# Rounded single-pass masks and gate sums, and the logits of two attention maps issued together, in a four-layer fp32 kernel

## The reference

```
logit[i, j] = q_i . k_j + c_i - c_j   for j <= i, masked above;  c = cumsum(log sigmoid(x w_f + b_f))
out = softmax(logit) v * silu(gate)
```

```
s[c] = scale * q[c] k[c]^T, masked above;  p[c] = softmax(s[c])
out = rmsnorm((p[0] - lam * p[1]) v) * (1 - lam0) * silu(z)
```

## Time and profile before

| | |
|---|---|
| median of 3 runs | 3882.92 us |
| the 3 runs | 3876.78, 3882.92, 3889.24 us |
| profiled execution, its time | 3884.34 us |
| profiled execution, its span | 3882.5 us |
| mean granted clock of TensorE | 0.961 |
| TensorE busy (matmul) | 3566.0 us, 92% |
| VectorE busy | 2130.9 us, 55% |
| ScalarE busy | 1293.7 us, 33% |
| instructions | 43173 |

### The profile page before, as it was taken

How to read it: one execution, slowest core, us unless ns; L and a number is a source line. 1 busy time by engine, 2 the same in 40 slices (tenths; PEclk the granted TensorE clock), 3 DMA queues, 4 the chain that set the end, 5 groups by cost and what they waited for, 6 DMA issues and landing times.

```text
span 3882.5 us, 43173 instructions
## 1 busy us (share of the span) xinstructions
PE 3566.0 (92%) x16018; PEld 2837.7 (73%) x16018; DVE 2130.9 (55%) x3127; ACT 1293.7 (33%) x2014; POOL 150.5 (4%) x100
## 2 busy tenths in 40 slices
PE   7899999978889999999989999998899999999899
PEld 6677777757667888878877777686677877677667
DVE  6655545555555555534343665476655466566664
ACT  4233323334323223333232224424333223432432
POOL 2000000000002000000031000000002000000000
PEclk9899999989989999999999999999999999999899
DMA  4233334445555555655543443334346343334345
GB/s 151 94 115 115 104 118 140 152 149 180 177 200 198 181 167 184 202 173 195 171 149 104 139 141 121 108 125 149 127 138 232 116 154 130 103 120 148 127 133 190
DMA packets 286129, 574.59 MB, mean 148 GB/s; under 512 B 61392, under 2 KB 101088, under 8 KB 285408
## 3 DMA queue, kind: packets, MB, share of 16 engines
q1 hardware_dynamic: 285920, 571.83, 44.2%
HBM read 440.65 MB, written 131.07 MB: 147 GB/s over the span
## 4 chain that ended last, share of the span: by engine, by line
PE 45%; issue 22%; DVE 16%; ACT 7%; DMA 6%; DVEq 2%; POOLq 1%; SPq 1%; ACTq 0%
PE bank L541 29%; PE bank L540 9%; DVE weights_low L466 4%; ACT weights_high L393 3%; DMA arena<-in_s_bc 2%; DVE arena L1947 1%; POOLq L452 1%; ACT arena L1889 1%; PE bank L2224 1%; PE bank L1064 1%; DVE arena L1811 1%; DMA arena<-fm_b 1%; DMA residual_in<-x_part 1%; DVE act_low L524 1%; PE bank L972 1%
## 5 line engine op out<-in xcount | busy, mean ns | idle before, releaser
L541 PE MATMUL bank<-act_high,weights_high 128*128 128x512 f32 x3584 | 1464.9, 409 | 62.4 <-DVE stream_out L513 27.5
L541 PE MATMUL bank<-act_low,weights_high 128*128 128x512 f32 x3584 | 1428.2, 398 | 0.0
L466 DVE TENSOR_TENSOR weights_low<-weights_raw,weights_high 128x1024 fp32r<-128x1024 f32 x528 | 656.7, 1244 | 1282.2 <-ACT weights_high L393 1279.9
L393 ACT ACTIVATE weights_high<-weights_raw 128x1024 fp32r<-128x1024 f32 x528 | 557.8, 1057 | 1608.2 <-PE bank L541 1336.5
L541 PE MATMUL bank<-act_high,weights_low 128*128 128x512 f32 x3584 | 964.6, 390 | 0.0
L541 PEld LDWEIGHTS bank<-act_high,weights_high 128*128 128x128 f32 x3584 | 696.7, 194 | 232.3 <-issue 38.6
L541 PEld LDWEIGHTS bank<-act_low,weights_high 128*128 128x128 f32 x3584 | 694.6, 194 | 142.4 <-issue 3.6
L541 PEld LDWEIGHTS bank<-act_high,weights_low 128*128 128x128 f32 x3584 | 673.9, 188 | 140.9
L540 PE MATMUL bank<-weights_high,act_high 128*128 128x512 f32 x640 | 257.7, 403 | 23.1 <-DVE stream_out L479 18.0
L540 PE MATMUL bank<-weights_high,act_low 128*128 128x512 f32 x640 | 252.5, 395 | 0.0
L2021 DVE SCALAR_TENSOR_TENSOR residual_in<-residual_in,arena 128x512 f32<-128x512 f32 x240 | 180.3, 751 | 20.2 <-issue 1.2
(11 more groups left out here) (314 smaller groups left out, 3043.7 us busy)
## 6 DMA issues: line engine op xcount, KB each, us to landing
weights_raw<-in_w_all SPq DMA_DIRECT2D x528, 512.0 KB, 3.4
convert_in<-mix SPq DMA_DIRECT2D x80, 256.0 KB, 4.0
fm_b<-stream_out SPq DMA_DIRECT2D x72, 256.0 KB, 2.3
mix<-arena SPq DMA_DIRECT2D x64, 256.0 KB, 4.2
x_part<-stream_out SPq DMA_DIRECT2D x48, 256.0 KB, 2.2
residual_in<-x_part SPq DMA_DIRECT2D x12, 1024.0 KB, 6.4
x<-stream_out SPq DMA_DIRECT2D x48, 256.0 KB, 2.6
convert_in<-x SPq DMA_DIRECT2D x48, 256.0 KB, 3.9
```

The lines of the kernel that those rows point to most:

```text
L393: e.activation(WH[:, t % 3, :], RAW[:, t % 3, :], ACT.Copy).then_inc(wh_ready, 1)
L466: e.tensor_tensor(WL[:, t % 3, :], RAW[:, t % 3, :], WH[:, t % 3, :].bitcast(F32), ALU.subtract).then_inc(wl_ready, 1)
L541: return e.matmul(bank[s][:, :], a[:, s * P:(s + 1) * P], h, start=start, stop=stop)
```

## The change

- The mask and the identity that carries it get rounded copies (`CAUSAL_R`, `IDENT_R`, type fp32r), made once by two ScalarE copies in the third unit; TensorE waits for them there. The mask's fill value becomes -2^100, which rounding keeps. All mask matmuls use the copies.
- The gate sums are kept on partitions 64 to 71 and 96 to 103 instead of 32 to 39, and stage `forget` splits them: rounded sums on the first group of partitions, the remainder on the second (`fx_cr`). A rounded selector for each head (`fx_head`) takes the place of the matrix of ones, so the product picks the head's row and adds both parts in one fp32r matmul. The multiplication L1441 and the semaphore step "row" go, and one of two memsets.
- In the differential attention both maps' q by k of a block are issued one behind the other, then both masks.
- Storage: `fx_cr` and `fx_head` lie in the buffer of the small weights, whose next filling waits for the last `fox` logits; the rotary tables are loaded into the start of `at_w`.

The diff:

```diff
@@ constants
-NEG = -1e30
+NEG = -2.0 ** 100
-        CAUSAL = sb("causal", [P, P])
+        IDENT_R = sb("ident_rounded", [P, P], F32R)
+        CAUSAL_R = sb("causal_rounded", [P, P], F32R)
...
@@ small_act
+            if i == 1:
+                e.wait_ge(*fx_p.at("lc", 7))
             e.activation(SMW[:, :, 0:64], small_raw, ACT.Copy).then_inc(*sm_a.mark("high"))
@@ fox: steps and buffers
-        fx_d = steps("fx_dve", "row m3 m2 m0 p3 p2 p0 m1 p1 mix")
+        fx_d = steps("fx_dve", "m3 m2 m0 p3 p2 p0 m1 p1 mix")
-        fx_row, fx_cum = A(L), A(L)
+        fx_cum = A(L)
-        FR = slice(32, 40)
+
+        FR, LOW = slice(64, 104), slice(96, 104)
+
+        fx_head, fx_cr = SMW[:, 0:8, :], two_d(SMW[:, 8:12, :])
@@ forget_dve
-            e.memset(fx_row, 0.0)
             e.memset(fx_one, 1.0)
...
             e.tensor_tensor_scan(fx_cum[FR, :], fx_one[FR, :], fx_t1[FR, :], 0.0, ALU.mult, ALU.add)
+            e.drain()
+            e.tensor_scalar(fx_cr, SMO[:, :], 0.0, None, ALU.mult)
+            e.drain()
+            e.tensor_copy(fx_cr[FR, :], fx_cum[FR, :])
+            e.tensor_copy(fx_head, fx_pick.rearrange("p (h o) -> p h o", o=1).broadcast_to([P, 8, P]))
+            e.drain()
+            e.tensor_tensor(fx_cr[LOW, :], fx_cum[LOW, :], fx_cr[LOW, :].bitcast(F32), ALU.subtract)
             e.drain().then_inc(*fc_d.mark("done"))
@@ fox_pe
                 e.matmul(out[:, :n], fx_q[:, b * P:n], fx_k[:, :n], start=True, stop=False)
-                e.matmul(out[:, :n], ONES[:, :], fx_row[:, :n], start=False, stop=False)
-                return e.matmul(out[:, b * P:n], IDENT[:, :], CAUSAL[:, :], start=False, stop=True)
+                e.matmul(out[:, :n], fx_head[:, h, :], fx_cr[:, :n], start=False, stop=False)
+                return e.matmul(out[:, b * P:n], IDENT_R[:, :], CAUSAL_R[:, :], start=False, stop=True)
...
-            e.wait_ge(*fx_d.at("row", h))
+            if h == 0:
+                e.wait_ge(*fc_d.at("done"))
@@ fox_dve
-            if h:
-                e.wait_ge(*fx_p.at("lc", h - 1))
-            else:
-                e.wait_ge(*fc_d.at("done"))
-            e.tensor_scalar(fx_row[FR, :], fx_cum[FR, :], fx_pick[FR, h:h + 1], None, ALU.mult).then_inc(*fx_d.mark("row"))
@@ attention
-        at_cos, at_sin = A(TB, 32), A(TB, 32)
+
+        at_cos, at_sin = (at_w[:, 0, 128 * n:128 * n + 128].rearrange("p (b d) -> p b d", b=TB) for n in range(2))
@@ att_pe
-            def logits(b, c, out):
-                w, r = (b + 1) * P, slice(64 * c, 64 * c + 64)
-                e.matmul(out[:, :w], at_q[r, b * P:w], at_k[r, :w], start=True, stop=False)
-                return e.matmul(out[:, b * P:w], IDENT[:, :], CAUSAL[:, :], start=False, stop=True)
+
+            def logits(b, outs):
+                w = (b + 1) * P
+                for c, out in enumerate(outs):
+                    r = slice(64 * c, 64 * c + 64)
+                    e.matmul(out[:, :w], at_q[r, b * P:w], at_k[r, :w], start=True, stop=False)
+                return [e.matmul(out[:, b * P:w], IDENT_R[:, :], CAUSAL_R[:, :], start=False, stop=True) for out in outs]
...
-            for c in range(2):
-                logits(3, c, mid[c]).then_inc(*p.mark(f"l3{c}"))
-            for c in range(2):
-                logits(2, c, mid[2 + c])
-                logits(0, c, mid[2 + c][:, 3 * P:]).then_inc(*p.mark(f"l2{c}"))
+            for c, mm in enumerate(logits(3, mid[0:2])):
+                mm.then_inc(*p.mark(f"l3{c}"))
+            logits(2, mid[2:4])
+            for c, mm in enumerate(logits(0, [x[:, 3 * P:] for x in mid[2:4]])):
+                mm.then_inc(*p.mark(f"l2{c}"))
...
-            for c in range(2):
-                mm = logits(1, c, mid[c])
-            mm.then_inc(*p.mark("l1"))
+            logits(1, mid[0:2])[1].then_inc(*p.mark("l1"))
@@ constants, ScalarE and TensorE at the third unit
                 if t == 2:
                     e.wait_ge(const_in, 80)
+                    e.activation(IDENT_R[:, :], IDENT[:, :], ACT.Copy)
+                    e.activation(CAUSAL_R[:, :], OUTB[:, 3, 0:P], ACT.Copy).then_inc(mask_ready, 1)
...
                 if t == 2:
                     e.wait_ge(const_in, 80)
+                    e.wait_ge(mask_ready, 1)
                 unit_pe(e, t)
```

More of the change, by code:

```diff
@@ L222, in build @@
         TRI = sb("tri", [P, P])
-        CAUSAL = sb("causal", [P, P])
+        IDENT_R = sb("ident_rounded", [P, P], F32R)
+        CAUSAL_R = sb("causal_rounded", [P, P], F32R)
         GAIN = sb("norm_gains", [P, 6, KT])
         GLUB = sb("glu_bias", [P, KT])
-        ARENA_N = 20040
+        ARENA_N = 19920
         ARENA = sb("arena", [P, ARENA_N])
@@ L256, in build @@
         out_stored, xr_in, zr_in = sem("out_stored"), sem("xr_in"), sem("zr_in")
-        const_in, gain_in = sem("const_in"), sem("gain_in")
+        const_in, gain_in, mask_ready = sem("const_in"), sem("gain_in"), sem("mask_ready")
         cv_in = [sem(f"cv_in{c}") for c in range(4)]
@@ L2543, in _ @@
             weights_sp(e, 2)
-            for dst, src in ((IDENT, "ident"), (TRI, "tri"), (CAUSAL, "causal"), (ONES, "ones"), (GLUB, "glu_b")):
-                e.dma_start(dst[:, :], I[src]).then_inc(const_in, 16)
+            for dst, src in ((IDENT[:, :], "ident"), (TRI[:, :], "tri"), (OUTB[:, 3, 0:P], "causal"), (ONES[:, :], "ones"), (GLUB[:, :], "glu_b")):
+                e.dma_start(dst, I[src]).then_inc(const_in, 16)
             for n in BY_SLOT[0]:
@@ L2676, in layout @@
     fb = np.zeros((P, 8), np.float32)
-    fb[32:40, 0] = v["fox_f_b"][0]
+    fb[64:72, 0] = fb[96:104, 0] = v["fox_f_b"][0]
     out["fox_b"] = fb
     pick = np.zeros((P, 8), np.float32)
-    pick[32:40] = np.eye(8)
+    pick[64:72] = pick[96:104] = np.eye(8)
     out["fox_pick"] = pick
     fold = np.zeros((P, P), np.float32)
-    fold[32:40, 32:40] = fold[96:104, 32:40] = np.eye(8)
+    for n in (64, 96):
+        fold[32:40, n:n + 8] = fold[96:104, n:n + 8] = np.eye(8)
     out["fox_fold"] = fold
```

## The result

The changed kernel takes 3842.09 us (median of 4 runs, 3841.32 to 3842.57), the kernel before 3879.85 us beside it (4 runs, 3874.81 to 3889.24): ratio 0.990, interval 0.988 to 0.992.

The account below looks back on a forecast made before the run. TensorE was taken as the bound, busy 92% of the span and holding 45% of the chain. Gains and losses 17.3 + 4.3 + 0.5 - 2.5 - 0.3 = 19.3 us, so 3884.3 - 19.3 = 3865.0 us; range 3854 to 3875.

Parts of the forecast that it names:

- the term 4.32: Differential attention, per head: both maps' q by k products counted one after the other, 2 x 2.16 us.
- half a product gained: Differential attention, going from one map's rows to the other's: the favourable bound, while nothing was charged.
- 17.3: Differential attention, TensorE: gain in us over both layers, six heads at 2.41 and two capped at 1.4.
- 0.3 us of copies: Third unit: two added ScalarE copies of 128x128, taken as 0.3 us lost, bounds 0 and 0.6.
- The sums: Forgetting attention's gate sums on VectorE, near 577 us: added instructions paid in full, 2.5 us lost.
- The rival: Differential attention: two maps' products partly overlap, three records instead of four, 6.5 us more gain, 3858.5 us; chance 0.22.
- The narrow pass: Mask matmuls: one rounded pass of 128 columns taken at 0.11 us, replacing an fp32 pair of 0.22.
- The rival that it costs 0.22: Both attentions: a rounded 128-column pass is no cheaper than the fp32 pair, 3871.3 us; chance 0.18.
- Height changes: Differential attention: each change between 64 and 128 rows costs about 0.20 us; 16 per head become 8.
- Head 0: Differential attention, first head of each layer: VectorE's own queue limits the gain, capped at 1.4 us a layer.
- 4.3 + 0.5 us: Forgetting attention: 4.3 us gained from logits of heads 1, 2 and 3, 0.5 from removing L1441.
- heads 4 to 7: Forgetting attention: shorter logits there only lengthen TensorE's waits, so no gain was counted.

Follow-up runs that it names:

- order undone: The changed kernel with the old issue order in the differential attention, rounded masks and gate sums kept: 3873.54 us, ratio 0.999.
- the two tripled kernels: Each differential-attention mask issued three times: on rounded masks alone in the old order, 3893.26 us; on the changed kernel in the new order, 3847.31 us.

## Why the prediction was wrong

**The step that failed** is the term 4.32 in "Head: 4.32 + 8 x 0.11 + 8 x 0.20 = 6.80". It puts the two maps' products one behind the other, 2 x 2.16, and their overlap at nothing ("half a product gained" stood among the bounds only). They run side by side and take 2.16. To charge nothing for the change of rows was right. Counted with measured terms a head is 2.16 + 4 x (0.06 + 0.11) + 8 x 0.20 = 4.44 us, measured 4.44; forecast 6.80. So 2.16 of the miss are the products and 0.20 the mask passes. The two attention stretches gave 33 to 35 us where 17.3 stood, the order alone 28 of them, and that kernel gained 24 of the 38 us in all.

**How much of the miss that is.** The sum stood at 19.3 us and the profiles differ by 41.8. Of the 22.5 between them 15.9 lie in the two attention stretches. Another 8.5 is what the stretches outside the two attentions (start, 1143 to 2667, 2909 to 3551) gave together in this pair of profiles, 4.0 in the second; but for 0.3 us of copies no step of mine spoke of them, and no part of the forecast can claim them. The sums and the forgetting attention came out 1.6 us short of the forecast.

**The rival had the mechanism and half its size.** I let only the first record of the second map run during the second of the first. The x4 rows show all four records within the time of two. The rule of the Trainium skill that the rival cited (page "TensorE: Matmul & The Clock Gate", section "Part 3: Packing small matmuls — row/col tiling"), that matmuls on different row groups run concurrently, is what the traces show here, in full: 1.06 us for both maps, 1.05 for one, and 1.70 where the rows were the same. I had made a number from the caution and not from the rule. With full overlap the sum would have been 3884.3 - 19.3 - 2 x 6.5 = 3852.0, still 10 us above the result.

**The narrow pass** costs 0.06 us and not 0.11 when it stands once between products. The 0.11 exists, as the price of each further pass in line, the second of a pair with it (0.37 - 0.20 = 0.17 for two). The rival that it costs 0.22 is refuted.

**Height changes** at 0.20, eight a head: right, by the 4.44 above.

**Head 0** was capped at 1.4 a layer. From the first logits of head 0 to those of head 1 it was 57.87 and 57.72 us; it is 55.70 and 57.60 in one profile of the changed kernel, 57.02 and 55.49 in the other, a gain of 1.3 on average. TensorE waits 1.93 us for L2400 there. Right in kind and size; the two small gains are those of the heads behind which the clock fell.

**Forgetting attention.** I put 4.3 + 0.5 us on the path. The logits of head 1 gave 2.08 us (blocks 3, 2 and 0 2.52 instead of 4.12, block 1 0.61 instead of 1.09), near the 1.98 of the sum. The 9.6 us from 582 to 769, followed unit by unit, come to 1.0 before the first logits of head 0, 0.8 with head 0 (0.5 of it L1441), 3.1 with head 1, 0.6 with head 2 and 4.1 with head 3. So heads 0 and 2 gave about what I had read, nothing and 0.74, and heads 1 and 3 more than their logits hold. By the estimate that rest, and the 1.0 ahead of head 0, is the clock (4.4 us in all). Before, it falls to 1.2 GHz for 3.4 us at 666 and at 752, behind the logits of heads 1 and 3:

```profile
666.50:669.50 3.00, 3.00 (x11) 2.52 (x10) 2.47 (x3) 1.08 (x2) 0.00 (x0) 0.50 0.49 165
752.00:755.00 3.00, 3.00 (x12) 2.71 (x13) 2.72 (x3) 1.08 (x2) 0.00 (x0) 0.50 0.34 93
```

All seven traces with fp32 sums have both falls, and none of the seven with rounded sums has either. For heads 4 to 7 I had said that shorter logits only lengthen a wait, and that is what they did: 8.0 us less work and 8.9 us more waits. The 6.8 us that this stretch lost are again the clock, 85.3 us at 1.2 GHz instead of 71.7; in the five other profiles with rounded sums and changed order it lost 3.5 to 7.7 with 10 to 17 us more at that level, in the one with the old order 1.7 with 3.4 more. From 552 to 1143 us the changed kernel gained 0.7 us in one profile and 0.5 in the other, where 4.8 - 2.5 = 2.3 stood: near it by luck, since some 4 us came from the clock and 5 to 6 went to it. The experiment without this part puts its worth at 8 to 10, with wide intervals. Why the falls are where they are stays open.

**The sums** were put at 2.5 us and cost 2.05. The four instructions are as listed, 0.43, 0.42, 0.69 and 0.69, some 2.5 with the drains; but VectorE's idle time ahead of the next instruction shrank from 0.85 to 0.36, which was not in the sum.

**What was not in the prediction**: some 4 us from 2193 to 2326 us and 2 to 5 from 1143 to 2193, where nothing of the change lies. From 1143 to 2193 the clock estimate covers most of the 5.4 and half of the 2.2. From 2193 to 2326 it covers 1.5; the rest is 2.5 to 3.0 us that TensorE waits less. It waits there for ScalarE (10.7 us before, 8.2 after), ScalarE for VectorE and VectorE, in part, for loads of `fm_b` (4.4 us before, 3.5 after). Every kernel with rounded mask passes waits 1.9 to 3.1 us less there, those with the storage alone or with the copies do not. Why is open. The loss of 5.2 and 3.9 us from 2909 to 3551 in the changed kernel goes with 13.7 and 17.1 us more at 1.2 GHz, more than in any of the other eleven profiles (at most 10.2), which have -1.6 to +1.7 there. How far the clock's falls differ by chance from one execution to the next is open.

**The clock.** No step spoke of it. In the old order the rounded masks gave 1.3 us a head and the clock took it back, with the masks alone more than that. The work of the two attention stretches nearly adds up: 28 us from the order, 10 from the masks alone, 36 from both. The times do not: a change whose order alone brings 24 us (ratio 0.9937), and whose rest alone brings 3, hardly clear of nothing (order undone, 0.9993), brings 37 to 39 with both. The falls are shown by the rows. That outside head 0 they need the old order is shown by the count above and by the two tripled kernels. What in that order brings the clock down is open: the number of passes is not it, and products side by side are not needed to avoid it, since the kernel with two products of one map in line has no fall either.

## What to carry over

Matmuls that use different halves of the rows and different banks should be issued one behind the other, with nothing of full height between; the second then costs nothing, and two products on the same rows get nothing from it. Price the pair by the longer one, and say so if you halve a rule out of caution. A shorter pass is worth its time only while the clock holds: look at the granted clock of the unit behind the edit, and test parts in pairs, since they need not add up (24 and 3 us alone, 37 to 39 together). Before a stretch's gain or loss is put down to an edit, take from it the waits and the time at the lower clock, and compare waits over the same window.

## What was unexpected on the chip

- Two fp32 products of two records each, on rows 0 to 63 and 64 to 127, take 1.06 us together for 512 columns, 0.85 for 384, 0.42 for 128 and 0.63 for 256, each with one change of height; one alone takes 1.05, 0.84, 0.41 and 0.63.
- Rounded masks in the old order: the granted clock is 0.50 (1.2 GHz) for some 3 to 10 us in or behind the logits of 22 of 24 heads, in the one shown after 8 us at 1.00 in which TensorE never waited. With fp32 masks, or with two products in line, it stays at 1.00 behind heads 1 to 3, even with three times the masks.
- The clock's falls move with edits elsewhere: two at 666 and 752 us are in all seven traces with fp32 gate sums and in none of the seven with rounded ones.
- A rounded pass of 128 columns takes 0.06 us alone between products and 0.11 for each further one in line.
